# Seven products for the embedding gates too, one bank rule for all panels, and reordered norm ends, experts' loop and third block's start

## The chip, the cores and the metric

The kernel runs on one core of a Trainium2 chip, in fp32. The metric is the device time of one execution, in microseconds. A core has TensorE (PE, matrix products into the 8 banks of PSUM), VectorE (DVE), ScalarE (ACT), GpSimd (POOL), a sync engine (SP) that issues transfers, and 16 DMA engines.

## What is computed

x is 256 tokens by 1024. Three blocks follow each other; cut to what matters here:

```python
# block 1, two layers
for i in range(2):
    mix = ssd_shortconv_layer_mixer(x, ...) if i == 0 else sliding_window_attention(x, ...)
    x = layer_norm(ALPHA * x + mix, ...)
    x = layer_norm(ALPHA * x + (silu(x @ w_gate[i]) * (x @ w_up[i])) @ w_down[i], ...)
    gate = sigmoid(x @ w_ple_gate[i] + b_ple_gate[i])
    x = x + (p[i] @ w_ple[i]) * gate
# block 2: RWKV-7 and stick-breaking attention, then a mixture of 32 experts, 4 for each token
x = x + gate1 * mixed
x = x + gate2 * moe_ffn(rms_norm(x, norm2_g) * (1 + scale2) + shift2, ...)
# block 3: two kinds of attention behind one input projection
h = rms_norm(x, g_pre) * (1 + scale) + shift
proj = h @ w_in
...
```

## The kernel before

x stays in SBUF, transposed: 8 tiles of 128 channels by 256 tokens. The weights are streamed once from HBM. SP brings panels of 1 MB (8 tiles of 128 channels by 256 columns) into a ring of 6 slots, and `linear` (L326) walks over them. A pair of output tiles (256 columns) of a normal panel is 16 products of 128x128 weights by 256 tokens, 8 for each tile, in one bank each; the profile shows a product of fp32 as two records.

**Seven products.** `SevenProducts` (L524 on) computes a panel as a 2x2 block product with seven multiplications in place of eight. Each multiplication is 4 products of 128x128 by 128 tokens (8 records). The order is 1, 5, 7, 6, 2, 3, 4; 1, 6, 5 and 7 go to the four quarters of the panel's first bank, 2, 3 and 4 to the second. GpSimd makes four sums of weights for a panel (`sums`, L585 to L590), VectorE four differences of activations (`turn`, L596 to L601), ScalarE copies the first quarter (L606), and VectorE combines: L612, L613 and L615 from the first bank, L618 from the second, which counts `combined` up. Only then are the two banks free. This form is used for ffn_up (22 pairs, the first one of each layer normal) and ffn_dn (3 panels of input channels for each of 4 pairs), in both layers. `wait_bank` (L374 on) waits, ahead of the first product of a panel, for both of its banks. The banks of a seven-product panel came from a table:

```python
SETS = ((0, 1), (2, 6))
bank = seven.SETS[n % 2][c] if seven is not None and pairs[q][0] in seven.names else (2 * q + c) % banks
```

with banks = 3 in the first block. The embedding gates, ple_g0 and ple_g1 (4 pairs each), use normal products.

**Order around a norm.** `linear` advances other programs between its tiles: what a program yields is the tile behind which it goes on. `LayerNorm` (L1085) follows the tiles of ffn_dn: VectorE adds x0 to x4 (L1168), TensorE sums them over the partitions by a product with ones, VectorE centers by this first mean (L1175, L1178, L1180), ScalarE squares (L1148), and behind the last pair VectorE adds x5 + x6 (L1184) and reduces six squares (L1186), before the last tile's addition (L1114). TensorE sums (L1127 to L1137) and VectorE reads the mean (L1190), then scales by L1204.

**The experts.** `mixture_of_experts` (L2745) works on one expert at a time, 12 panels of 1 MB: 8 that widen (L3071) and 4 that narrow (L3101), as 6 pairs. Pairs lie in 8 slots: the first TWICE = 2 pairs of an expert have a slot for even and one for odd experts, the other four have one. A turn of the TensorE loop is: widen u, scatter u-1, gather u+2, narrow u. Scattered results are added by VectorE to `acc` (L2840, 4 additions of 512 columns). While the routing is computed TensorE ends with idle products of a constant (L2870). Behind the last expert `ClosingNorm` (L2681) adds gate times `acc` to x (L2697) and makes the sum of squares for the third block.

**Third block.** `third_block` (L3606) waits for the finished norm: `NormTail` scales (L268) and shifts (L274) the 8 tiles into h, and `linear` starts behind each.

## Time and profile before

| | before |
|---|---|
| median of 3 runs | 2394.82 us (2394.03 to 2396.35) |
| profiled execution, its own time | 2397.78 us |
| its span, first to last instruction | 2395.9 us |
| granted TensorE clock, mean | 0.987 of full speed |
| TensorE busy | 2261.8 us, 94% |
| HBM read | 616.63 MB, 258 GB/s over the span |

The span is the profiler's; the device time of the same execution is 1.9 us longer, and sums are made against that. The first block lasts until about 920, the second until 2130, of which the experts take 1198 to 2120, and the third to the end. In rows of stretches the number behind each busy time is a count of instructions. In a timeline a gap in brackets is the engine's idle time before the row, with what ended it. Granted clock 1.00 is 2.4 GHz.

### The profile page before, as it was taken

To read this page: it belongs to the slowest core of one execution; us is meant where nothing else is said; L and a number is where in the kernel's file an instruction comes from. 1 tells how busy PE (TensorE), PEld (TensorE's weight loads), DVE (VectorE), ACT (ScalarE), POOL (GpSimd) and SP (SyncE) were. 2 spreads that over 40 slices of the span, in tenths; PEclk is the share of its full clock that TensorE was granted. 3 is DMA by queue.
4 is the path that set the end of the run, shared out by engine and by line. 5 is a ranking of instruction groups with operands and counts; after the bars stand their busy time and mean duration, and the time that the engine had idled before them with its cause. 6 is when DMAs were issued, how large, how long until landed. Compare 5 with 4: busy or idle time off the path is not lost. (4 is left out here: it accounts for less than half of the span.)

```text
span 2395.9 us, 35084 instructions
## 1 busy us (share of the span) xinstructions
PE 2261.8 (94%) x14543; PEld 1537.5 (64%) x14543; DVE 890.1 (37%) x1790; ACT 419.3 (18%) x898; POOL 417.1 (17%) x343
## 2 busy tenths in 40 slices
PE   8999999989899989999999999999999999989998
PEld 7888799977699977877733333333333333358886
DVE  4242565634444653626422222222322222253222
ACT  1210121014211013224111111111111111123331
POOL 0110498700088830011000000000000000000000
PEclk9999899999999989999999999999999999999999
DMA  6334644454854444310699999999999999943322
GB/s 263 132 124 141 213 167 160 163 191 181 317 211 161 160 170 154 124 37 2 283 376 428 428 428 428 428 428 428 428 428 428 428 428 428 428 194 124 143 71 88
DMA packets 61005, 619.28 MB, mean 258 GB/s; under 512 B 6784, under 2 KB 8064, under 8 KB 12288
## 3 DMA queue, kind: packets, MB, share of 16 engines
q1 hardware_dynamic: 59184, 611.08, 63.9%
q10 hardware_dynamic: 1712, 6.63, 0.8%
q8 instruction: 83, 1.36, 0.2%
q14 instruction: 26, 0.21, 0.0%
HBM read 616.63 MB, written 1.05 MB: 258 GB/s over the span
## 5 line engine op out<-in xcount | busy, mean ns | idle before, releaser
L431 PE MATMUL ps<-x_res,ring 128*128 128x256 f32 x1216 | 284.2, 393 | 24.0 <-ACT x_res L1157 15.4
L431 PEld LDWEIGHTS ps<-x_res,ring 128*128 128x128 f32 x1216 | 236.3, 197 | 64.8 <-issue 16.8
L3071 PE MATMUL ps<-expert_ring,moe_xg 128*64 128x512 f32 x1024 | 229.0, 594 | 25.7 <-DMA expert_ring<-we_dram 25.7
L3071 PE MATMUL ps<-ring,moe_xg 128*64 128x512 f32 x1024 | 227.9, 594 | 5.1 <-DMA ring<-we_dram 5.1
L3101 PE MATMUL ps<-expert_ring,mix_y 128*64 128x512 f32 x1024 | 226.8, 596 | 0.0
L3133 DVE TENSOR_SCALAR mix_y<-ps 128x512 f32<-128x512 f32 x32 | 22.1, 691 | 454.5 <-PE ps L3071 454.5
L3389 POOL COPY third_mla_kv<-third_lat 32x256 f32<-32x256 f32 x8 | 3.5, 457 | 1055.4 <-ACT third_mla_kv L658 1055.3
L3071 PEld LDWEIGHTS ps<-expert_ring,moe_xg 128*64 128x64 f32 x1024 | 71.5, 137 | 172.2 <-issue 124.6
L431 PE MATMUL ps<-third_h,ring 128*128 128x256 f32 x768 | 176.6, 387 | 5.2 <-ACT third_h L274 4.3
L3071 PEld LDWEIGHTS ps<-ring,moe_xg 128*64 128x64 f32 x1024 | 72.0, 137 | 150.9 <-issue 125.1
L431 PEld LDWEIGHTS ps<-third_h,ring 128*128 128x128 f32 x768 | 148.0, 194 | 28.1 <-issue 6.6
L3101 PEld LDWEIGHTS ps<-expert_ring,mix_y 128*64 128x64 f32 x1024 | 70.5, 137 | 133.4 <-issue 133.4
L3114 ACT ACTIVATE mix_y<-mix_y 128x512 f32<-128x512 f32 x32 | 20.2, 630 | 695.6 <-DVE mix_y L3133 695.6
L431 PE MATMUL ps<-mix_arena,ring 128*128 128x256 f32 x416 | 96.2, 389 | 4.3 <-ACT mix_arena L274 4.3
L586 POOL TENSOR_TENSOR ring<-ring 128x512 f32<-128x512 f32 (+1 forms) x66 | 99.9, 1514 | 0.0
L585 POOL TENSOR_TENSOR seven_weights<-ring 128x512 f32<-128x512 f32 (+1 forms) x66 | 86.0, 1304 | 71.8 <-PE ps L414 64.3
L431 PEld LDWEIGHTS ps<-mix_arena,ring 128*128 128x128 f32 x416 | 79.7, 194 | 17.3 <-issue 6.1
L588 POOL TENSOR_TENSOR seven_weights<-seven_weights,ring 128x512 f32<-128x512 f32 (+1 forms) x66 | 90.2, 1366 | 0.0
L414 PE MATMUL ps<-x_res,ring 128*128 128x128 f32 x672 | 89.0, 276 | 0.0
L414 PE MATMUL ps<-seven_x_turned,ring 128*128 128x128 f32 x672 | 88.8, 275 | 0.0
L414 PE MATMUL ps<-seven_x_turned,seven_weights 128*128 128x128 f32 x672 | 88.8, 275 | 0.0
L3148 DVE COPY moe_ytok<-ps 128x512 f32<-128x512 f32 x32 | 22.1, 692 | 176.1 <-PE ps L3101 176.1
(592 smaller groups left out, 3319.8 us busy)
## 6 DMA issues: line engine op xcount, KB each, us to landing
expert_ring<-we_dram SPq DMA_DIRECT2D x128, 2048.0 KB, 22.0
ring<-we_dram SPq DMA_DIRECT2D x64, 2048.0 KB, 24.5
ring<-w_in_dram SPq DMA_DIRECT2D x55, 1024.0 KB, 4.9
ring<-ffn_up_dram SPq DMA_DIRECT2D x44, 1024.0 KB, 4.9
ring<-ada_dram SPq DMA_DIRECT2D x36, 1024.0 KB, 4.9
ring<-w_out_dram SPq DMA_DIRECT2D x16, 1024.0 KB, 4.9
ring<-ffn_dn_dram SPq DMA_DIRECT2D x16, 1024.0 KB, 4.9
ring<-ple_g_dram SPq DMA_DIRECT2D x8, 1024.0 KB, 5.6
```

The costliest lines, as they stand in the source:

```text
L414: mm = pe.matmul(core.ps[:, bank, at:at + P], seven.weight(w, f, half, product, p), seven.moving(panel, sources[panel], k0, half, product, ...
L431: mm = pe.matmul(core.ps[:, bank_of[n, c], 0:TOK], w[:, k * PANEL + c * P:k * PANEL + c * P + P], sources[panel](k0 + k), start=(k0 + k == ...
L585: pool.tensor_tensor(s1, a21, a22, ALU.add).then_inc(summed.sem, 1)
L586: pool.tensor_tensor(a21, a11, a21, ALU.subtract).then_inc(summed.sem, 1)
L588: pool.tensor_tensor(s2, s1, a11, ALU.subtract).then_inc(summed.sem, 1)
L3071: mm = pe.matmul(ps[out, bank, :], xg[:, j % 4, j // 4, :], w[:, bank * D + at:bank * D + at + 512], start=False, stop=(j == 7))
L3101: mm = pe.matmul(ps[out, 2, :], hidt[:, at_k:at_k + S], w[:, i * D + at:i * D + at + 512], start=False, stop=(k == DT - 1))
L3114: act.activation(sg[:, :], glu[:, :], ACT.Sigmoid, scale=SWIGLU_ALPHA).then_inc(sig_ready.sem, 1)
L3133: dve.tensor_scalar(glu[:, :], ps[:, 0, :], SWIGLU_LIMIT, None, ALU.min).then_inc(glu_ready.sem, 1)
L3148: dve.tensor_copy(ytok[:, :], ps[:, 2, :]).then_inc(copied.sem, 1)
L3389: pool.tensor_copy(kv[64:96, t, :], lat[64:96, 3, :]).then_inc(*inc("keyed"))
```

## The change

- `SETS` is gone. The banks of unit n (a panel by seven products, or a normal pair) are (2n) mod 3 and (2n + 1) mod 3, also in the names with seven products. Where two such panels follow each other, the second bank of the later is the first bank of the earlier.
- Pairs 1 to 3 of ple_g0 and ple_g1 go by seven products, 6 panels, with turned activations of their own.
- GpSimd starts the weight sums of the first fast panel of ffn_up0, ffn_up1, ple_g0 and ple_g1 only when VectorE's four differences are there.
- In the norms of ffn_dn (`split`) the first mean is that of x0 to x3, the reduction of six squares stands behind the centering and no longer behind the last pair, x4 to x7 are summed by TensorE directly, and the five filling products stand together behind them.
- Experts: nine slots of pairs (TWICE = 3) in place of eight (the memory of `acc` goes to it); the results are added straight into x with their gate, in 8 instructions of 256 columns; expert 0 is widened in the routing's block, with the loads for its slots' successors; the loop's turn is narrow u, widen u+1. `widen` and `narrow` have the instructions of the old loop body. `ClosingNorm` is gone.
- Third block: `UnscaledStart`. The first four tiles are computed from x times gain, unscaled (with one more column, the shift, so 257), and multiplied by the root's inverse afterwards by VectorE, then shifted by ScalarE. The sum of squares is four ones products in the middle of the second tile. h for the later tiles is made meanwhile.

```diff
-            bank = seven.SETS[n % 2][c] if seven is not None and pairs[q][0] in seven.names else (2 * q + c) % banks
+            bank = raw.BANKS[2 * q + c] if raw is not None and 2 * q + c < raw.COUNT else (2 * n + c) % banks
...
-                    for k in range(kn):
+                    if raw is not None and t < raw.COUNT:
+                        for m, k in enumerate(raw.ORDER):
+                            raw.before(pe, t, m)
+                            mm = pe.matmul(core.ps[:, bank_of[n, c], 0:raw.WIDTH], w[:, k * PANEL + c * P:k * PANEL + c * P + P], raw.moving(k),
+                                           start=(m == 0), stop=(m == DT - 1))
+                    for k in range(kn if raw is None or t >= raw.COUNT else 0):
+                        if raw is not None and t == raw.COUNT:
+                            raw.wait(pe, k)
...
-    SETS = ((0, 1), (2, 6))
...
+        name, j = core.stream[i][0:2]
+        if j == self.first_pair[name] > 0:
+
+            pool.wait_ge(self.turned.sem, self.turned.at(4 * self.groups[name, 0] + 4))
...
+        if self.split:
+            self.wait(pe, "centered", 2)
+            for t in range(4, 8):
+                if t == 6:
+                    self.wait(pe, "squares_added_up", 1)
+                    pe.matmul(ps[:, 5, 0:TOK], ones, self.run.shift[:, :], start=True, stop=False)
+                if t >= 6:
+                    core.wait_tile(pe, self.first + t)
+                mm = pe.matmul(ps[:, 4, TOK:], ones, x[:, t, :], start=(t == 4), stop=(t == 7))
+            mm.then_inc(*self.inc("mean"))
+            for t in (6, 7):
+                self.wait(pe, "squared", t - 3)
+                mm = pe.matmul(ps[:, 5, 0:TOK], ones, sq[:, t, :], start=False, stop=(t == 7))
+            mm.then_inc(*self.inc("power"))
+            self.fill(pe, 5)
+            return
...
+        summed = 4 if self.split else 5
+        for t in range(1, summed):
+            yield self.first + t
+            core.wait_tile(dve, self.first + t)
+            add = dve.tensor_tensor(run.offset[:, :], x[:, 0, :] if t == 1 else run.offset[:, :], x[:, t, :], ALU.add)
+            if t < summed - 1:
...
+        if self.split:
+            self.wait(dve, "squared", 2)
+            dve.tensor_reduce(run.shift[:, :], run.sq[:, 0:6, :].rearrange("p t n -> p n t"), AX,
+                              ALU.add).then_inc(*self.inc("squares_added_up"))
+        yield self.first + 6
+        if not self.split:
+            self.add_last(dve)
...
+        turn_order = [("ffn_up0", 0), *(("ffn_dn0", k0) for k0 in range(0, FF_T, KG)), ("ple_g0", 0),
+                      ("ffn_up1", 0), *(("ffn_dn1", k0) for k0 in range(0, FF_T, KG)), ("ple_g1", 0)]
+
+        def groups(name):
+            return {k0: n for n, (of, k0) in enumerate(turn_order) if of == name}
+        parts_fast = {name: (1, turned_x, None, groups(name)) for name in ("ffn_up0", "ple_g0", "ffn_up1", "ple_g1")}
...
+class UnscaledStart:
+
+
+    ORDER, BANKS, COUNT, WIDTH = (0, 1, 4, 5, 2, 3, 6, 7), (0, 1, 2, 6), 4, TOK + 1
+    SUM_BANK = 7
...
+    def before(self, pe, t, n):
+        if t == 0:
+            if n == 0:
+                self.at(pe, "columns", 1)
+            self.at(pe, "gained", n + 1)
+        if (t, n) == (1, 4):
+            self.at(pe, "halved", 1)
+            for i in range(4):
+                mm = pe.matmul(self.core.ps[:, self.SUM_BANK, 0:TOK], self.core.m("ones"), self.sq[:, i, :], start=(i == 0), stop=(i == 3))
+            mm.then_inc(*self.inc("summed"))
...
+        for k in self.ORDER:
+            part = core.ps[:, 2 + k // 2, k % 2 * TOK:k % 2 * TOK + TOK]
+            dve.scalar_tensor_tensor(out=x[:, k, :], in0=part, scalar=gate[:, k:k + 1], in1=x[:, k, :], op0=ALU.mult,
+                                     op1=ALU.add).then_inc(*self.inc("kept"))
+        self.at(dve, "kept", DT)
+        dve.tensor_tensor(sq[:, 0:4, :], x[:, 0:4, :], x[:, 0:4, :], ALU.mult).then_inc(*self.inc("squared"))
+        self.at(dve, "squared", 2)
+        dve.tensor_tensor(sq[:, 0:4, :], sq[:, 0:4, :], sq[:, 4:8, :], ALU.add).then_inc(*self.inc("halved"))
+        self.at(dve, "summed", 1)
+        dve.tensor_scalar(rstd[:, :], core.ps[:, self.SUM_BANK, 0:TOK], 1.0 / D, RMS_EPS, ALU.mult, ALU.add).then_inc(*self.inc("var"))
+        self.at(dve, "rooted", 1)
+        dve.reciprocal(rstd[:, :], rstd[:, :]).then_inc(*self.inc("inverse"))
+        self.at(dve, "inverse", 1)
+        for t in range(self.COUNT):
+            if t == 2:
+                for half in range(2):
+                    part = slice(4 * half, 4 * half + 4)
+                    dve.tensor_tensor(self.out[:, part, :], self.xg[:, part, 0:TOK], bcast(rstd[:, :].unsqueeze(1), [P, 4, TOK]),
+                                      ALU.mult).then_inc(*self.inc("h_scaled"))
+            core.wait_product(dve, t)
+            bank = core.bank_of_tile(t)
+            dve.tensor_copy(self.added[:, t:t + 1], core.ps[:, bank, TOK:TOK + 1])
+            dve.tensor_tensor(self.first_tiles[t], core.ps[:, bank, 0:TOK], rstd[:, :], ALU.mult).then_inc(*self.inc("scaled"))
...
+        for n, k in enumerate(self.ORDER):
+            self.at(act, "kept", n + 1)
+            act.activation(self.xg[:, k, 0:TOK], x[:, k, :], ACT.Copy, scale=core.gain[:, k:k + 1]).then_inc(*self.inc("gained"))
+        act.activation(self.sq[:, 4:8, :], x[:, 4:8, :], ACT.Square).then_inc(*self.inc("squared"))
+        self.at(act, "var", 1)
+        act.activation(core.rstd[:, :], core.rstd[:, :], ACT.Sqrt).then_inc(*self.inc("rooted"))
...
-                part = acc[:, 4 * i + 2 * q:4 * i + 2 * q + 2, :]
                 dve.wait_ge(scattered.sem, scattered.at(u * 4 + (n + 1)))
-                dve.tensor_tensor(part, part, ps[:, 2 + 2 * i + q, :].rearrange("p (k n) -> p k n", n=TOK),
-                                  ALU.add).then_inc(added.sem, 1)
+                for t in range(2):
+                    k = 4 * i + 2 * q + t
+                    ins = dve.scalar_tensor_tensor(out=x[:, k, :], in0=ps[:, 2 + 2 * i + q, t * TOK:t * TOK + TOK], scalar=gate[:, k:k + 1],
+                                                   in1=x[:, k, :], op0=ALU.mult, op1=ALU.add)
+                ins.then_inc(added.sem, 1)
...
-                    keep_busy(12)
+                    widen(pe, 0, 0, 0)
...
+                    load(sp, 0, twice, 0, 2)
+                    load(sp, 0, opened, 1, 1)
...
+                load(sp, 0, range(4, PAIRS), 1, 1)
+                load(sp, 1, twice, 1, 3)
+                load(sp, 1, once, 0, 2)
+                with sp.Fori(2, AHEAD) as v:
+                    load(sp, v * 2 - 2, twice, 0, v * 2)
+                    load(sp, v * 2 - 2, once, 1, v * 2 - 1)
+                    load(sp, v * 2 - 1, twice, 1, v * 2 + 1)
+                    load(sp, v * 2 - 1, once, 0, v * 2)
...
+                last = last_pair(pe)
+                with pe.Fori(0, last) as v:
+                    narrow(pe, v * 2, v, 0)
+                    widen(pe, v * 2 + 1, v, 1)
+                    narrow(pe, v * 2 + 1, v, 1)
+                    widen(pe, v * 2 + 2, v + 1, 0)
+                narrow(pe, last * 2, last, 0)
+                widen(pe, last * 2 + 1, last, 1)
+                narrow(pe, last * 2 + 1, last, 1)
+                scatter(pe, last * 2 + 2)
...
-PANELS, PAIRS, TWICE, AHEAD = 12, 6, 2, 9
...
+PANELS, PAIRS, TWICE, AHEAD = 12, 6, 3, 9
...
-        norm = NormTail(core, h, x, lambda k: core.gain[:, k:k + 1], lambda k: shift[:, k:k + 1])
+        start = UnscaledStart(core, s, h, [lat[:, m, :] for m in range(4)])
```

Three places show the new order. The first is TensorE at ple_g0, in the second of its pairs (`x_res` is x, `seven_x_turned` the differences, `seven_weights` the sums, `ring` the panel). The columns are line, operation, output<-inputs, shape, what it waits for, and how often it comes. Before:

```order
L431 MATMUL ps<-x_res,ring 128x256 [waits seven_combined,panel_loaded3]
L431 MATMUL ps<-x_res,ring 128x256 x7
L431 MATMUL ps<-x_res,ring 128x256 [waits act_evac]
L431 MATMUL ps<-x_res,ring 128x256 x7
```

With the change:

```order
L424 MATMUL ps<-x_res,ring 128x128 [waits seven_combined,act_evac,panel_loaded4]
L424 MATMUL ps<-x_res,ring 128x128 x3
L424 MATMUL ps<-seven_x_turned,seven_weights 128x128 [waits seven_summed]
L424 MATMUL ps<-seven_x_turned,seven_weights 128x128 x3
L424 MATMUL ps<-seven_x_turned,ring 128x128 [waits seven_summed]
L424 MATMUL ps<-seven_x_turned,ring 128x128 x3
L424 MATMUL ps<-seven_x_turned,seven_weights 128x128 [waits seven_summed]
L424 MATMUL ps<-seven_x_turned,seven_weights 128x128 x3
L424 MATMUL ps<-x_res,ring 128x128 x4
```

Sixteen products of 256 tokens have become seven groups of four; the wait for the combination stands at the first product, while the second bank is first written by the fifth group (`x_res` with `ring`, x4 in one row). Inside ffn_up and ffn_dn the rows read the same before and after, only the count that `seven_combined` must have reached is that of the panel before, no longer of the one before that.

The second is VectorE at the end of ffn_dn0, from the last combination that the first mean comes before to the reading of the mean. Before:

```order
L1175 TENSOR_SCALAR ln_shift<-ps 128x256 [waits layer_signal28,dve_evac]
L1178 TENSOR_TENSOR x_res<-x_res,ln_shift 128x768 [waits dve_chain]
L1178 TENSOR_TENSOR x_res<-x_res,ln_shift 128x768
L1180 SCALAR_TENSOR_TENSOR x_res<-x_res,ln_shift 128x512
L612 TENSOR_TENSOR seven_second<-seven_part,ps 128x128 [waits seven_copied,dve_chain]
L613 TENSOR_TENSOR seven_part<-seven_second,ps 128x256 [waits dve_chain]
...
L1114 TENSOR_TENSOR x_res<-x_res,seven_stage 128x256 [waits seven_combined]
L1184 TENSOR_TENSOR ln_offset<-x_res 128x256 [waits layer_signal29,dve_evac]
L1186 TENSOR_REDUCE ln_shift<-ln_sq 128x256 [waits layer_signal30]
L1114 TENSOR_TENSOR x_res<-x_res,seven_stage 128x256 [waits seven_combined]
L1190 TENSOR_SCALAR ln_offset<-ps 128x256 [waits layer_signal31]
```

With the change:

```order
L1225 TENSOR_SCALAR ln_shift<-ps 128x256 [waits layer_signal28,dve_evac]
L1228 TENSOR_TENSOR x_res<-x_res,ln_shift 128x768 [waits dve_chain]
L1228 TENSOR_TENSOR x_res<-x_res,ln_shift 128x768
L1230 SCALAR_TENSOR_TENSOR x_res<-x_res,ln_shift 128x512
L1233 TENSOR_REDUCE ln_shift<-ln_sq 128x256 [waits layer_signal30,dve_chain]
L633 TENSOR_TENSOR seven_second<-seven_part,ps 128x128 [waits seven_copied]
L634 TENSOR_TENSOR seven_part<-seven_second,ps 128x256 [waits dve_chain]
...
L1137 TENSOR_TENSOR x_res<-x_res,seven_stage 128x256 [waits seven_combined] x2
L1240 TENSOR_SCALAR ln_offset<-ps 128x256 [waits layer_signal31]
```

The reduction (L1186, now L1233) has moved ahead of the combination of the first panel of the last pair, and the addition of x5 and x6 (L1184) is gone.

The third is TensorE from the end of the routing to the experts' loop. Before:

```order
L2909 MATMUL ps<-route_onehot,mat 1x17
L2870 MATMUL ps<-mat 128x128 [waits layer_signal26]
L2870 MATMUL ps<-mat 128x128 x11
L2858 UNCONDITIONAL_BRANCH
L3050 UNCONDITIONAL_BRANCH [waits barrier_Pool_Activation_PE_DVE_SP_release]
L2776 TENSOR_LOAD moe_unit_int
L2776 ISA x2
...
L3066 MATMUL ps<-bias_parts,moe_pick 64x512 [waits expert_xg_ready,expert_expert_picked]
L3066 MATMUL ps<-bias_parts,moe_pick 64x512 x3
```

With the change:

```order
L3076 MATMUL ps<-route_onehot,mat 1x17
L2951 MATMUL ps<-bias_parts,moe_pick 64x512 [waits layer_signal26,expert_xg_ready,expert_expert_picked]
L2951 MATMUL ps<-bias_parts,moe_pick 64x512 x3
L2956 MATMUL ps<-ring,moe_xg 64x512 [waits expert_pair0]
L2956 MATMUL ps<-ring,moe_xg 64x512 x7
...
L2956 MATMUL ps<-expert_ring,moe_xg 64x512 [waits expert_pair3]
L2956 MATMUL ps<-expert_ring,moe_xg 64x512 x7
L3022 UNCONDITIONAL_BRANCH
L3209 UNCONDITIONAL_BRANCH [waits barrier_Pool_Activation_PE_DVE_SP_release]
L2876 TENSOR_LOAD moe_unit_int
...
L2931 MATMUL ps<-moe_selt,moe_ytok 128x256 [waits expert_added]
```

The idle products (L2870) have become the widening of expert 0 (4 pairs, 8 products each), and the loop begins with a scatter (L2931).

## Rows read from the trace of the kernel before

**Rows 1.** The page, busy time of each engine.

```profile
PE 2261.8 (94%) x14543; PEld 1537.5 (64%) x14543; DVE 890.1 (37%) x1790; ACT 419.3 (18%) x898; POOL 417.1 (17%) x343
```

**Rows 2.** Windows: stretch, length, busy of each engine, PEclk, DMA share, GB/s.

```profile
275.00:406.00 131.00, 131.00 (x1175) 130.97 (x1174) 67.11 (x114) 24.89 (x45) 112.55 (x80) 1.00 0.49 168
1300.00:1400.00 100.00, 97.36 (x489) 35.91 (x489) 26.49 (x63) 11.03 (x16) 0.00 (x0) 1.00 1.01 428
458.00:461.00 3.00, 0.29 (x3) 0.14 (x2) 2.75 (x4) 0.00 (x0) 3.00 (x3) 1.00 0.55 161
461.00:465.00 4.00, 4.00 (x20) 3.95 (x21) 3.93 (x4) 0.81 (x1) 3.92 (x3) 0.57 0.34 141
1190.00:1210.00 20.00, 17.07 (x104) 9.60 (x106) 4.73 (x23) 2.11 (x3) 0.00 (x0) 1.00 0.46 177
2120.00:2126.40 6.40, 4.51 (x16) 2.53 (x16) 5.07 (x11) 3.25 (x8) 0.00 (x0) 1.00 0.34 140
```

**Rows 3.** The chain that ended last: start us, us, engine, line, count.

```profile
2151.15 13.81 PE ps L431 x64
```

**Rows 4.** Timeline, ffn_up0: start us, us, engine, line, op, names, shapes, count.

```profile
400.14 1.06 PE L414 MATMUL ps<-x_res,ring 128*128 128x128 f32 x8
400.34 0.56 DVE L618 TENSOR_TENSOR seven_stage<-seven_part,ps 128x384 f32<-128x384 f32 x1 [1.24 <-PE ps L414]
406.39 1.06 PE L414 MATMUL ps<-first_arena,ring 128*128 128x128 f32 x8
```

**Rows 5.** Timeline, norm at the end of ffn_dn0.

```profile
481.01 0.42 DVE L1114 TENSOR_TENSOR x_res<-x_res,seven_stage 128x256 f32<-128x256 f32 x1
481.81 2.74 DVE L1186 TENSOR_REDUCE ln_shift<-ln_sq 128x256 f32<-128x1536 f32 x1
484.60 0.70 PE L1132 MATMUL ps<-ln_shift,mat 128*128 128x256 f32 x2 [1.96 <-DVE ln_shift L1186]
488.96 0.42 DVE L1190 TENSOR_SCALAR ln_offset<-ps 128x256 f32<-128x256 f32 x1 [4.08 <-PE ps L1137]
```

**Rows 6.** Timeline, end of the routing and first product of expert 0.

```profile
1193.79 2.95 PE L2870 MATMUL ps<-mat 128*128 128x128 f32 x24
1198.37 0.62 PE L3066 MATMUL ps<-bias_parts,moe_pick 96*64 96x512 bf16 x4 [1.64 <-issue]
```

**Rows 7.** Timeline, middle of ffn_up0 and its step to ffn_dn0.

```profile
368.87 1.06 PE L414 MATMUL ps<-x_res,ring 128*128 128x128 f32 x8
378.35 0.55 DVE L618 TENSOR_TENSOR seven_stage<-seven_part,ps 128x384 f32<-128x384 f32 x1
414.38 0.55 DVE L618 TENSOR_TENSOR seven_stage<-seven_part,ps 128x384 f32<-128x384 f32 x1
```

**Rows 8.** Timeline, centering in ffn_dn0.

```profile
462.70 3.41 DVE L1178 TENSOR_TENSOR x_res<-x_res,ln_shift 128x768 f32<-128x768 f32 x2
```

**Rows 9.** Timeline, scaling ahead of ffn_up0, of ple_g0 and of ffn_up1.

```profile
257.25 10.61 DVE L1204 SCALAR_TENSOR_TENSOR x_res<-x_res,vec,norm_rstd 128x256 f32<-128x256 f32 x8
275.08 1.05 PE L414 MATMUL ps<-x_res,ring 128*128 128x128 f32 x8
494.99 3.25 DVE L1204 SCALAR_TENSOR_TENSOR x_res<-x_res,vec,norm_rstd 128x256 f32<-128x256 f32 x8
504.79 0.47 ACT L659 ACTIVATE first_arena<-ps,vec 128x256 f32<-128x256 f32 x1 [2.98 <-PE ps L431]
653.47 4.27 DVE L1204 SCALAR_TENSOR_TENSOR x_res<-x_res,vec,norm_rstd 128x256 f32<-128x256 f32 x8
```

**Rows 10.** Timeline, end of the experts and start of the third block.

```profile
2117.87 2.00 PE L2831 MATMUL ps<-moe_selt,moe_ytok 64*128 64x256 f32 x16 [0.87 <-DVE moe_ytok L3148]
2119.76 0.88 DVE L2697 SCALAR_TENSOR_TENSOR x_res<-moe_acc,modulations,x_res 128x256 f32<-128x256 f32 x2
2127.36 1.75 DVE L2721 RECIPROCAL norm_rstd<-norm_rstd 128x256 f32<-128x256 f32 x1 [0.48 <-ACT norm_rstd L2707]
2146.44 0.38 ACT L658 ACTIVATE third_lat<-ps 128x256 f32<-128x256 f32 x1 [3.07 <-PE ps L431]
```

323 lines of the change are left out of this document (152 added, 171 removed).

## The prediction, before the change ran

> **What bounds the kernel now.** I read the busy times first: TensorE works 94% of the span, VectorE 37%, GpSimd 17% [rows 1]. So nearly every microsecond that TensorE gains or loses is one of the program, unless TensorE waits for weights. The table of stretches shows the two regimes [rows 2]. In the first block (275 to 406) TensorE is busy 131.00 of 131.00 at clock 1.00 and the DMA share is 0.49: TensorE is the bound, and any wait between two panels is paid in full. In the experts (1300 to 1400) the DMA share is 1.01 at 428 GB/s: the weights are the bound, and work of 2 or 3 us that is moved there costs nothing. The third block (the chain's one run of 64 products, 13.81 us [rows 3]) is TensorE's again. The sum is made against the profiled execution, 2397.78 us; the median of the runs shown, 2394.82, is 2.96 lower. About 0.2%, 4.8 us, is what a measurement can tell from no change.
>
> **A, the banks.** A panel by seven products fills two banks. Before, two neighbours had four different banks, so TensorE waited for the combination of the panel before last. Now the second bank of a panel is the first of the panel before it, and both waits stand ahead of the first product. The next panel starts at 400.14, but VectorE's last combination of the panel before starts only at 400.34 and takes 0.56 [rows 4]. So each boundary gets 0.20 + 0.56 = 0.76, plus the way of the signal from VectorE to TensorE, 0.05 (a reduction of 2.74 from 481.81 ends at 484.55, the product that waits for it starts at 484.60 [rows 5]), plus a first weight load that nothing hides: two products alone take 0.70 there, where in a run of 24 each takes 2.95 / 24 = 0.12 at 128 columns [rows 5, 6]; I estimate 0.10. That is 0.9 each; bounds 0.75 (signal and load hidden) and 1.05 (both doubled). Boundaries: per layer 20 inside ffn_up, 1 to ffn_dn, 11 inside ffn_dn and 2 between the new gate panels, 34; two layers 68, less one that the modulation work hides in ffn_up1: 67 × 0.90 = **+60.3**.
>
> **B, VectorE late.** In the middle of ffn_up VectorE also turns half of the hidden vector, ahead of the combination. There the combination ends at 378.35 + 0.55 = 378.90, 10.03 after the panel began at 368.87 [rows 7]; with signal and load 10.18. A panel takes 6.25 (400.14 to 406.39 [rows 4]), and the next would now end its own stall at 0.90 + 6.25 = 7.15. TensorE stands still 3.0, of which 0.90 is counted: 2.1, four times, **+8.4**. At the step to ffn_dn the combination ends at 414.93, 8.54 after 406.39 [rows 4, 7]: 8.69 − 7.15 = 1.54, of which 0.64 is new, twice, **+1.3**.
>
> **C, the clock.** Behind the stretch 458 to 461, where TensorE worked 0.29 of 3 us, the next 4 us run at a granted clock of 0.57: 0.43 × 4 = 1.7 lost [rows 2]. I charge this to the four stalls of 3.0: **+6.8**, bounds 0 and 6.8.
>
> **D, the norm at the end of ffn_dn.** VectorE's sums of squares move from the last slot to the one before. Centering starts 1.7 into the panel (462.70 [rows 8], the panel at 461.0 [rows 2]) and takes 3.41; then the two late tiles (a third more, 1.1), what is left of the squares on ScalarE (0.25, estimated), the reduction of 2.74 [rows 5], the combination (1.2 and 0.55) and the signal, 0.15: 11.1, and the panel is over at 6.25. That stall is 4.9 instead of 0.9: 4.0 more, and 1.7 of clock; what goes is the old wait for the fifth tile, 2.7 and its 1.7 of clock [rows 2]. Twice +1.3: **+2.6**. What it buys comes at the very end. The last tile's addition starts at 481.01, the reduction then holds VectorE for 2.74 and TensorE starts behind it at 484.60; the mean is read at 488.96 [rows 5]. Now the last addition ends near 481.9, two ones products remain (0.6) and the mean is read near 482.75: 6.2 earlier, twice, **−12.4**. Adding x4 to x7 on TensorE costs nothing on VectorE, whose sums are hidden by TensorE's tiles; if that cover went it would be 0.35 a product, half of the 0.70 of two [rows 5].
>
> **E, the gates.** Six panel pairs go from 32 products at 13.81 / 64 = 0.216, 6.91 [rows 3], to 6.25 [rows 4]: 0.66 each, **−4.0**. Their turning on VectorE lies under the normal first pair, GpSimd's first sum behind it; both are there before the second product. Were they late, TensorE would wait for them on VectorE's and GpSimd's time, and GpSimd is idle there.
>
> **F, weight sums wait for the activation sums.** At ffn_up0 the scaling starts at 257.25, takes 10.61 beside GpSimd's sums, and the first fast panel starts at 275.08, 17.8 later. At ple_g0, with GpSimd idle, it takes 3.25 from 494.99, and the pair's last product ends just ahead of the evacuation at 504.79, 9.6 later [rows 9]. So **−8.2** there; in ffn_up1 the scaling took 4.27 [rows 9], 0.8 more than it must, **−0.8**. The sums themselves start later, under the normal pair of 6.91, and are needed only one product, 6.25 / 7 = 0.89, into the fast one; that cover is what hides them.
>
> **G, the experts.** From 1190 to 1210 the DMA share is 0.46 [rows 2]: 20 × 0.54 = 10.8 us of a bandwidth-bound phase not used, because the ring was full and freed only once the first expert was widened. A ninth pair of panels (2 MB at 428 GB/s, 4.9) can be loaded in that time, and widening starts where the idle products were, 4.4 to 4.6 earlier (1193.79 against 1198.37 [rows 6]), so slots free 4.4 earlier. Of the hole 1.6 stays; and since loads of expert 1 beyond the fourth pair wait for expert 0's narrowing, behind a barrier, a hole of about 2.7 opens: 10.9 − 4.3 = **−6.6**, bounds −3 and −10.9. Adding eight 256-column parts straight into x instead of four of 512 costs VectorE about 0.9 an expert, hidden by the DMA-bound loop (VectorE works 26.49 of 100 there [rows 2]); without that cover 32 × 0.9 = 29.
>
> **H, third block.** The last scatter (2117.87, 2.00) ends at 2119.87, and the fourth tile's product ends at about 2146.25, just ahead of its evacuation [rows 10]. Now: barrier 0.4, eight residuals of 0.44 (0.88 for two [rows 10]) to 2123.8; the unscaled products follow and tile 0 ends near 2125.8; three tiles of 3.46 (6.91 / 2) and four ones products, 1.73 (4 × 2 × 0.216), to 2138.0; the reciprocal (1.75 [rows 10]) runs beside them. With 1.9 for a slow clock behind the pause (0.43 × 4 as in C, rounded up, since the pauses are several), 2139.9: **−6.3**, bounds −4 and −7.5.
>
> **Sum:** 60.3 + 8.4 + 1.3 + 6.8 + 2.6 = 79.4; −12.4 −4.0 −9.0 −6.6 −6.3 = −38.3; net +41.1. 2397.78 + 41.1 = 2438.9, less 2.96: **2436**.
>
> **Rivals.**
> - *The boundary wait is hidden (faster).* The shared bank is written by the fifth of seven products only, 3.6 us in. If the wait did not hold the first product (the combination frees the bank earlier than the rows say, or products already queued cover it), A, B and C go: −38.3, 2356. It decides at 38.3 / 67 = 0.57 a boundary with B and C gone, or 0.29 with them. Against it: the order of instructions has the wait on the first product; [rows 4] give at least 0.76. Chance 0.04.
> - *The clock falls at every boundary.* An idle of 2.7 cost 1.7 afterwards [rows 2]. If 0.9 did so too, 67 × 1.7 = 114: 2550. Against it: from 2120 to 2126.4 TensorE worked only 4.51 of 6.40, in short pauses between its ones products, and the clock stayed 1.00 [rows 2]. The Trainium skill (TensorE: Matmul & The Clock Gate, A second HAM failure mode: psum-queue depth-cycling) tells of a kernel whose TensorE "micro-idles between MM groups" while it cycles through banks, and whose clock then oscillates; by it this rival would be the forecast. The stretch just quoted does not follow that rule, though it is only 6 us long. Chance 0.08.
> - *The repairs don't do what they are for.* The experts' start is bound by something else than the ring, and the third block's start by its pauses: G and H are 0, 2449. Chance 0.06.
>
> **How the numbers follow.** The forecast has 0.80; 0.02 is left for what I don't see. The low end takes A at 0.75 (−10), C at 0 (−6.8), G and H at their best (−5.5) and F and E exact: about 2412 with 2 for B. The high end takes A at 1.05 (+10), G and H at their worst (+5.9), and the norms' gain 3 less each (+6): 2458, rounded to 2460; the third rival lies inside. Left out are the clock (0.08), the hidden wait (0.04) and the rest. Slower by over 0.2%: 0.80 + 0.08 + 0.06 = 0.94; faster 0.04, same 0.02.
>
> **What the changed profile must show.** At each fast panel in ffn_up a wait of TensorE of about 0.9 on VectorE's last combination, some 67 times, and TensorE's busy share there at 0.87 instead of 1.00; four idles of 3.0 and two of 4.9 with a clock of about 0.6 behind them; the mean of ffn_dn's norm read 6 us sooner after the last product; the first scaling of ffn_up0 in 3.3; a DMA share near 0.8 in the 20 us before the experts' loop; the fourth tile of the third block 20 us behind the last scatter, not 26.4. I am wrong if TensorE runs through the boundaries, or if the clock is below 0.9 all through ffn_up.

## The result, and the profile after

The changed kernel takes **2439.19 us** in the median of 4 runs (2437.22 to 2441.01), the kernel before 2394.43 on the same chip: ratio 1.0187, 95% interval 1.017 to 1.0205, 44.8 us slower. Forecast: 2436, range 2412 to 2460. The profiled execution took 2439.19 (span 2437.4), 41.4 more than the profiled one of before; the sum had said 41.1.

Busy time of the engines on the page of after (span first), against [rows 1]:

```profile
span 2437.4 us, 35516 instructions
## 1 busy us (share of the span) xinstructions
PE 2256.9 (93%) x14663; PEld 1541.6 (63%) x14663; DVE 910.1 (37%) x1946; ACT 420.9 (17%) x905; POOL 437.7 (18%) x367
```

TensorE's busy time fell by 5 us while the span grew by 41.5: what was added is waiting. What TensorE waited for (columns: in total, times, longest):

```profile
engine line waited for: us in total, times, longest us
PE ps L424 <- DVE seven_stage L639: 63.1, 67, 5.1
PE ps L2956 <- DMA expert_ring<-we_dram: 25.0, 19, 1.6
```

The first line does not exist in the kernel before. 67 times is the number that the prediction counted; 52 of the waits are 0.74 long, the others 0.3 to 5.1. One boundary inside ffn_up0, and the one in the middle where VectorE is late (timeline, columns as in [rows 4], some rows between left out):

```profile
372.54 0.29 DVE L636 TENSOR_TENSOR seven_stage<-seven_part,ps 128x128 f32<-128x128 f32 x1
372.97 1.06 PE L424 MATMUL ps<-seven_x_turned,ring 128*128 128x128 f32 x8
374.07 0.55 DVE L639 TENSOR_TENSOR seven_stage<-seven_part,ps 128x384 f32<-128x384 f32 x1 [1.24 <-PE ps L424]
374.77 1.13 PE L424 MATMUL ps<-x_res,ring 128*128 128x128 f32 x8 [0.74 <-DVE seven_stage L639]
375.73 1.06 PE L424 MATMUL ps<-seven_x_turned,seven_weights 128*128 128x128 f32 x8
...
383.07 1.13 PE L424 MATMUL ps<-x_res,ring 128*128 128x128 f32 x8 [1.81 <-DVE seven_stage L639]
...
390.30 1.13 PE L424 MATMUL ps<-x_res,ring 128*128 128x128 f32 x8 [0.74 <-DVE seven_stage L639]
```

Without a wait the next panel would start 0.89 behind the last group, at 373.86. VectorE begins its last combination 0.21 later, needs 0.55, TensorE starts 0.15 behind its end, and the first group then takes 0.07 more (0.96 to the next, not 0.89): 0.98 for a boundary. Panels now come every 7.23 (383.07 to 390.30), not every 6.25 [rows 4]. The late one in the middle has 1.81 in place of 0.74.

The first row shows something more. L636 (L615 before) is the last instruction that reads the panel's first bank, the one that the next panel needs again. It ends at 372.83, a microsecond ahead of 373.86. What TensorE waits for is the counter `combined`, which goes up only behind the combination from the other bank.

That late place came out earlier than forecast. Of VectorE's four differences there, the last one and what GpSimd did beside it, before and after:

```profile
375.44 1.46 POOL L585 TENSOR_TENSOR seven_weights<-ring 128x512 f32<-128x512 f32 x1 [0.21 <-PE ps L414]
375.81 1.65 DVE L601 TENSOR_TENSOR seven_h_turned<-first_arena,seven_h_turned 128x512 f32<-128x512 f32 x1
```

```profile
380.80 0.69 DVE L622 TENSOR_TENSOR seven_h_turned<-first_arena,seven_h_turned 128x512 f32<-128x512 f32 x1
381.40 1.26 POOL L606 TENSOR_TENSOR seven_weights<-ring 128x512 f32<-128x512 f32 x1 [1.19 <-PE ps L424]
```

It takes 1.64 or 1.65 in all four such places of the kernel before, and 0.69 in all four of the changed one. At the place shown GpSimd now stands idle for 1.19, until TensorE has finished a panel whose buffer its sums need.

Stretches of after (columns as in [rows 2]):

```profile
266.00:410.00 144.00, 127.82 (x1107) 124.75 (x1106) 62.18 (x108) 24.40 (x43) 113.71 (x83) 1.00 0.45 151
384.00:390.00 6.00, 5.56 (x50) 5.37 (x49) 1.57 (x5) 0.28 (x1) 2.87 (x3) 1.00 0.24 102
486.80:491.90 5.10, 0.03 (x1) 0.00 (x0) 4.62 (x7) 0.85 (x2) 4.00 (x4) 1.00 0.58 206
491.95:495.95 4.00, 4.00 (x21) 4.00 (x22) 0.58 (x1) 0.00 (x0) 0.00 (x0) 0.57 0.02 4
801.40:805.40 4.00, 4.00 (x25) 4.00 (x26) 0.65 (x1) 0.22 (x1) 3.36 (x3) 0.66 0.48 203
2171.32:2175.32 4.00, 4.00 (x11) 3.21 (x12) 2.46 (x5) 3.60 (x8) 0.00 (x0) 0.57 0.08 30
```

ffn_up0 is busy 127.82 of 144 with the clock at 1.00 throughout, also behind the 1.81 us stall (384 to 390). It falls to 0.57 behind the 5.12 us stall in ffn_dn's last pair, and behind the pause of 2.99 ahead of the third block. It also falls behind one of the four late stalls, the second of ffn_up1, to 0.66:

```profile
801.32 1.13 PE L424 MATMUL ps<-x_res,ring 128*128 128x128 f32 x8 [2.10 <-DVE seven_stage L639]
...
810.17 1.13 PE L424 MATMUL ps<-x_res,ring 128*128 128x128 f32 x8 [0.74 <-DVE seven_stage L639]
```

This panel takes 8.85 instead of 7.23, 1.6 more. The long stall and the norm's end (timeline):

```profile
487.59 2.78 DVE L1233 TENSOR_REDUCE ln_shift<-ln_sq 128x256 f32<-128x1536 f32 x1 [0.38 <-ACT ln_sq L1187]
...
491.25 0.55 DVE L639 TENSOR_TENSOR seven_stage<-seven_part,ps 128x384 f32<-128x384 f32 x1
...
491.95 1.95 PE L424 MATMUL ps<-first_arena,ring 128*128 128x128 f32 x8 [5.12 <-DVE seven_stage L639]
493.68 1.92 PE L424 MATMUL ps<-seven_h_turned,seven_weights 128*128 128x128 f32 x8
...
505.76 0.55 DVE L639 TENSOR_TENSOR seven_stage<-seven_part,ps 128x384 f32<-128x384 f32 x1 [0.57 <-PE ps L424]
...
508.00 0.42 DVE L1240 TENSOR_SCALAR ln_offset<-ps 128x256 f32<-128x256 f32 x1 [0.89 <-PE ps L1160]
```

The mean is read 2.24 behind the start of the last combination; before it was 8.54 (the combination L618 started at 480.42, the mean is in [rows 5]). 6.3 us are won at each of the two ends.

The scaling ahead of ffn_up0 and ffn_up1, and the first fast panels behind them, against [rows 9] (and 663.42 for ffn_up1 before):

```profile
257.19 3.26 DVE L1254 SCALAR_TENSOR_TENSOR x_res<-x_res,vec,norm_rstd 128x256 f32<-128x256 f32 x8
...
265.35 1.05 PE L424 MATMUL ps<-x_res,ring 128*128 128x128 f32 x8
...
672.32 3.25 DVE L1254 SCALAR_TENSOR_TENSOR x_res<-x_res,vec,norm_rstd 128x256 f32<-128x256 f32 x8
...
682.99 1.16 PE L424 MATMUL ps<-x_res,ring 128*128 128x128 f32 x8
```

8.16 from scaling to panel in ffn_up0 (17.83 before), 10.67 in ffn_up1 (9.95 before).

The start of the third block, against [rows 10]:

```profile
2166.34 2.00 PE L2931 MATMUL ps<-moe_selt,moe_ytok 64*128 64x256 f32 x16 [0.87 <-DVE moe_ytok L3261]
...
2171.32 7.13 PE L439 MATMUL ps<-unscaled_x,ring 128*128 128x257 f32 x24 [2.99 <-ACT unscaled_x L2808]
...
2180.02 8.85 PE L439 MATMUL ps<-unscaled_x,ring 128*128 128x257 f32 x40
...
2188.70 3.62 PE L448 MATMUL ps<-third_h,ring 128*128 128x256 f32 x16
```

The fourth tile is done where the first product with h starts, at 2188.70. That is 20.4 behind the end of the last scatter (2166.34 + 2.00), where the forecast was 20.0; before it was 26.4. So 6.0 are won there. From the start of the scatter to the end of the span it is 271.1 us, before 278.0: 7.0 won.

From the first gather of the routing (1187.66 before, 1238.11 after) to the last scatter it is 930.2 before and 928.2 after: the turned loop with its ninth pair has won 2.0. The two kernels stand 50.5 apart at that gather, 48.5 at the scatter and 41.5 at the end.

### The profile page after: what moved, and what is told of

It is laid out like the page before. It is cut to its first block and busy times, and to the rows that moved or that the text cites. A ratio compares the mean times of both kernels' runs of the same rounds, so it can differ in the third digit from the quotient of the medians.

```text
span 2437.4 us, 35516 instructions
## 1 busy us (share of the span) xinstructions
PE 2256.9 (93%) x14663; PEld 1541.6 (63%) x14663; DVE 910.1 (37%) x1946; ACT 420.9 (17%) x905; POOL 437.7 (18%) x367
## 5 line engine op out<-in xcount | busy, mean ns | idle before, releaser
L2956 PE MATMUL ps<-expert_ring,moe_xg 128*64 128x512 f32 x1280 | 283.4, 594 | 25.3 <-DMA expert_ring<-we_dram 25.0
L448 PE MATMUL ps<-x_res,ring 128*128 128x256 f32 x1024 | 235.1, 389 | 18.9 <-ACT x_res L1196 10.3
L448 PEld LDWEIGHTS ps<-x_res,ring 128*128 128x128 f32 x1024 | 198.0, 196 | 49.3 <-issue 14.0
L2956 PEld LDWEIGHTS ps<-expert_ring,moe_xg 128*64 128x64 f32 x1280 | 89.8, 137 | 208.7 <-issue 160.4
L2956 PE MATMUL ps<-ring,moe_xg 128*64 128x512 f32 x768 | 170.1, 598 | 0.2
L448 PE MATMUL ps<-third_h,ring 128*128 128x256 f32 x704 | 160.1, 383 | 1.3 <-DVE third_h L3740 1.0
L448 PEld LDWEIGHTS ps<-third_h,ring 128*128 128x128 f32 x704 | 134.1, 192 | 21.2 <-issue 2.2
L424 PE MATMUL ps<-x_res,ring 128*128 128x128 f32 x768 | 104.8, 280 | 36.0 <-DVE seven_stage L639 36.0
L2956 PEld LDWEIGHTS ps<-ring,moe_xg 128*64 128x64 f32 x768 | 55.3, 138 | 106.3 <-issue 100.3
L424 PEld LDWEIGHTS ps<-x_res,ring 128*128 128x128 f32 x768 | 93.5, 192 | 43.8 <-issue 43.6
L2941 DVE SCALAR_TENSOR_TENSOR x_res<-ps,modulations,x_res 128x256 f32<-128x256 f32 x256 | 102.9, 474 | 0.0
L424 PE MATMUL ps<-first_arena,ring 128*128 128x128 f32 x528 | 74.2, 283 | 27.1 <-DVE seven_stage L639 27.1
```

The costliest lines, as they stand in the source:

```text
L424: mm = pe.matmul(core.ps[:, bank, at:at + P], seven.weight(w, f, half, product, p), seven.moving(panel, sources[panel], k0, half, product, ...
L448: mm = pe.matmul(core.ps[:, bank_of[n, c], 0:TOK], w[:, k * PANEL + c * P:k * PANEL + c * P + P], sources[panel](k0 + k), start=(k0 + k == ...
L2941: ins = dve.scalar_tensor_tensor(out=x[:, k, :], in0=ps[:, 2 + 2 * i + q, t * TOK:t * TOK + TOK], scalar=gate[:, k:k + 1], in1=x[:, k, :], ...
L2956: mm = pe.matmul(ps[out, bank, :], xg[:, j % 4, j // 4, :], w[:, bank * D + at:bank * D + at + 512], start=False, stop=(j == 7))
```

## The experiments

**The wait alone.** TensorE waits for the second bank only where it is first written:

```diff
                     wait_bank(pe, n, 0)
-                    wait_bank(pe, n, 1)
...
                     for product in seven.ORDER:
+                        if product == 2:
+                            wait_bank(pe, n, 1)
```

> The changed kernel, but TensorE waits for a panel's second bank only ahead of the fifth of its seven products, the first that writes it. Theory (the wait at the first product is the cost): the combination ends 0.76 after the panel's start and the fifth product comes 3.6 after it, so the 67 stalls of 0.74, the four late ones of 1.8 to 2.1 and most of the two of 5.1 at ffn_dn's last pair go; the bank rule itself costs nothing. 67 x 0.98 = 65.7, 6 for the late ones and about 7 for the two long ones: 2439 - 79 = 2360, and a panel takes 6.25 again. Rival (the three banks themselves are too few, since VectorE must read a bank while TensorE fills the next one): the stall moves to the fifth product and the time stays above 2400.

Measured: 2361.30 (2359.98 to 2363.79), ratio to before 0.9846 (0.9829 to 0.9862). Three waits are left of the 67:

```profile
PE ps L425 <- DVE seven_stage L640: 5.1, 3, 2.4
```

and the stretch of ffn_up0 is full again:

```profile
266.00:390.00 124.00, 123.93 (x1103) 123.46 (x1102) 63.81 (x106) 23.93 (x42) 113.11 (x82) 1.00 0.53 173
```

So the place of the wait cost 78 us, and with three banks and this wait the changed kernel is faster than the one before. The shared bank still costs something. The two longest of the three waits, 2.35 and 2.37, stand ahead of the fifth product in ffn_dn's last pair, where VectorE's reduction has come in between, and the clock falls behind them (timeline, then the stretch):

```profile
463.13 1.16 PE L425 MATMUL ps<-first_arena,ring 128*128 128x128 f32 x8 [2.35 <-DVE seven_stage L640]
464.13 1.75 PE L425 MATMUL ps<-first_arena,seven_weights 128*128 128x128 f32 x8
```

```profile
463.13:467.13 4.00, 4.00 (x23) 4.00 (x24) 1.67 (x4) 0.28 (x1) 0.00 (x0) 0.65 0.00 0
```

Another remedy was not tested: the wait left where it is, but for a signal of its own behind the last instruction that reads the first bank (372.83 in the rows above), in place of `combined`.

**Four banks.** The table of before in the changed kernel, for all names with seven products:

```diff
-            bank = raw.BANKS[2 * q + c] if raw is not None and 2 * q + c < raw.COUNT else (2 * n + c) % banks
+            bank = (raw.BANKS[2 * q + c] if raw is not None and 2 * q + c < raw.COUNT else
+                    ((0, 1), (2, 6))[n % 2][c] if seven is not None and pairs[q][0] in seven.names else (2 * q + c) % banks)
```

> The changed kernel with the old table of four banks for all names with seven products. Theory: what remains are the other parts, without any boundary: -65.7 for the stalls, -6 for the late ones, and the two long stalls at ffn_dn's last pair go whole (11.1 against 12.5 of two panels), 2 x 6: about 2355, a little under the late wait. Rival (the clock or VectorE's later work bounds these stages anyway): above 2390.

Measured: 2352.72 (2350.04 to 2355.28), ratio 0.9816 (0.9799 to 0.9832). TensorE waits for no combination. That is 8.6 us below the late wait on the same chip. In ffn_dn0's last pair, from its first product to the product with ones behind it, it is 21.44 us with the late wait and 17.22 here: 4.2 for the stall of 2.35 and its clock, in two layers 8.4. The same kernel once more, on the chip of the last group of runs:

> The changed kernel with four banks once more, on the chip of the three others, as their reference: 2353, between 2350 and 2357. If it falls outside of that, the differences to the runs on another chip are read with that error.

Measured: 2354.63 (2353.73 to 2356.98), ratio 0.9822 (0.9806 to 0.9839). No version of the study is measurably faster; it is 43 us below the kernel before (2397.67 on that chip) and 85 below the changed one. It is the base of the experiments that follow, called the base.

**The banks alone.** The kernel before, with one edit:

```diff
-            bank = seven.SETS[n % 2][c] if seven is not None and pairs[q][0] in seven.names else (2 * q + c) % banks
+            bank = (2 * n + c) % banks
```

> The kernel before with nothing changed but the bank rule, (2n + c) mod 3 for all panels. Theory: 63 boundaries (no fast gates) at 0.98, 61.7, and 6 for the late combinations, so 2394 + 68 = 2462, panels of 7.23. Rival (the stalls come from the other edits, the moved reduction and the weight sums that wait): near 2394.

Measured: 2467.34 (2466.41 to 2470.36), before 2397.38, +70.0; ratio 1.0289 (1.0272 to 1.0306).

```profile
PE ps L414 <- DVE seven_stage L618: 51.0, 61, 1.8
```

The stalls need neither the moved reduction nor the late sums. The loss was forecast at 68; 61 waits were found where 63 were expected.

**Weight sums at once.** The base, without GpSimd's new wait:

```diff
-        if j == self.first_pair[name] > 0:
-
-            pool.wait_ge(self.turned.sem, self.turned.at(4 * self.groups[name, 0] + 4))
```

> The changed kernel with four banks, but GpSimd does not wait for the activation sums. Theory: +9.7 at ffn_up0 where the scaling takes 10.6 again beside GpSimd, -0.7 at ffn_up1, and new overlaps of the same kind ahead of the fast gates in both layers, up to 7 each: between 2362 and 2376, 2369 if half of them overlap. Rival (the start of ffn_up0 is bound by ScalarE's shift or the weights and not by VectorE): within 2 us of 2353.

Measured: 2372.27 (2371.88 to 2377.90), 17.6 to 19.6 above the two runs of the base. The group of the scaling, of the changed kernel and of this one (columns: total busy, mean ns, idle before):

```profile
L1254 DVE SCALAR_TENSOR_TENSOR x_res<-x_res,vec,norm_rstd 128x256 f32<-128x256 f32 x32 | 13.0, 479 | 0.1
```

```profile
L1252 DVE SCALAR_TENSOR_TENSOR x_res<-x_res,vec,norm_rstd 128x256 f32<-128x256 f32 x32 | 33.0, 1100 | 0.1
```

One of them takes at least 472, in the median 1483 and at most 1533 ns (minimum, median and maximum):

```profile
L1252 DVE SCALAR_TENSOR_TENSOR x_res<-x_res,vec,norm_rstd x32: 472/1483/1533, 257.4 to 874.6; 128x256 f32<-128x256 f32 x32
```

The Trainium skill (SBUF — State Buffer, SBUF: two separate sides) says that a VectorE instruction with two inputs in SBUF and one of GpSimd that reads SBUF exclude each other for a whole instruction. The trace agrees: 1483 ns is about the length of one of GpSimd's additions, 1.45 us at this place.

In all the 32 instructions make 33.0 instead of 13.0 us of busy time, since with fast gates GpSimd sums beside the scaling at all four norms: the eight instructions take 9.99, 7.32, 7.35 and 8.32 instead of 3.26. At the two norms ahead of the gates that is 9.1 more, and the fast gates win 4 to 7 (below). By this estimate fast gates without the wait would be a loss; normal gates without it were not run.

**Norm ends of before**, in the base (the class `LayerNorm` of the kernel before; no other edit):

> The changed kernel with four banks and the norm ends of the kernel before. Theory: with four banks VectorE's moved work stalls nobody, so the norm ends are worth their whole gain here, twice 6.3 at the end plus 2.4 for the wait on the fifth tile and 1.7 of clock: 2353 + 21 = 2374. Rival (the moved reduction costs elsewhere what it saves): +13 or less, below 2366.

Measured: 2375.80 (2374.04 to 2378.34), 21.2 to 23.1 above the base. The whole gain is there once nobody waits for VectorE's moved work.

**Normal gates**, in the base (ple_g0 and ple_g1 taken out of the names with seven products, with their turns):

> The changed kernel with four banks and normal products for the embedding gates. Theory: six pairs at 6.91 instead of 6.25, +4.0: 2357. Rival (turning and sums around the gates cost what the seventh product saves): no change beyond 1.5 us.

Measured: 2359.77 (2354.64 to 2363.61). 5 to 7 above the base where 4.0 were expected; its runs spread over 9 us, so this confirms the sign, not the size.

**Loads in one order.** The changed kernel, with SP's order of the first loop in all loops:

```diff
                 def in_turn(v, before, even, odd):
-                    load(sp, v * 2 - 2, once, 1, before)
                     load(sp, v * 2 - 2, twice, 0, even)
-                    load(sp, v * 2 - 1, once, 0, even)
+                    load(sp, v * 2 - 2, once, 1, before)
                     load(sp, v * 2 - 1, twice, 1, odd)
+                    load(sp, v * 2 - 1, once, 0, even)
```

> The changed kernel, but SP issues the experts' loads in one order (three pairs with two slots first) through all loops; the changed kernel switches to the other order at expert 18, where the DMA share falls to 0.89 over 20 us at 1730. Theory: that hole is the switch, with three pairs held back behind one that is late; without it -2.5 to -2.9, 2436.5. Rival (an unrelated pause of the DMA engines): no change beyond 1 us, and a hole somewhere.

Measured: 2449.06 (2443.16 to 2454.97): slower by 10, the expectation was wrong. The stretch of the old hole, in the changed kernel and then here, and the end of the loop here:

```profile
1730.00:1750.00 20.00, 20.00 (x96) 6.53 (x92) 2.24 (x9) 0.00 (x0) 0.00 (x0) 1.00 0.89 365
```

```profile
1730.00:1750.00 20.00, 18.48 (x95) 6.61 (x91) 3.86 (x8) 0.63 (x1) 0.00 (x0) 1.00 1.00 426
2140.00:2170.00 30.00, 28.95 (x146) 10.51 (x142) 8.52 (x22) 2.42 (x4) 0.00 (x0) 1.00 0.82 344
```

The hole is indeed the switch, since it is gone (share 1.00). But it buys something: in this order the next expert's first three pairs are loaded ahead of the last three of the present one, TensorE still waits 1.5 for a pair of the last but one expert, and behind it the engines run dry (0.82) while TensorE works alone. From the first gather to the last it is 924.0 us, in the changed kernel 917.1. (This trace had the faster first widening, of which below; beside a trace with the same, the base's first with 914.3, it is 9.7 more.)

**The switch elsewhere.** The base with `AHEAD` = 3 (expert 6) and with `AHEAD` = 14 (expert 28), in place of 9 (expert 18):

> The changed kernel with four banks, and the experts' loads change their order at expert 6 instead of expert 18. Theory (the lead of three pairs has to be given back somewhere; a hole of 2.9 us at the switch is the price of the ninth pair, and it is the same wherever the switch stands once the slots are full): no change beyond 1.5 us, 2353, with the hole near expert 6. Rival (near the start the DMA engines wait for slots anyway, so that the two holes fall together): -2 to -3, 2350.

Measured: 2359.58 (2352.01 to 2363.06), 5 to 7 above the base, its fastest run level with it: neither the theory nor the rival. The trace is that of the fastest run. The hole came later than at the start, and larger than at expert 18 (31% of 20 us, 6.2; by the bytes, 261 instead of 428 GB/s, 7.8):

```profile
1280.00:1300.00 20.00, 19.33 (x102) 7.54 (x100) 8.19 (x21) 2.42 (x4) 0.00 (x0) 1.00 0.69 261
```

> The changed kernel with four banks, and the loads change their order at expert 28. At expert 18 the switch left a hole of 2.9 us, at expert 6 one of 6.2, with no switch at all 7 us were lost at the end. Theory (TensorE needs 27.6 us for an expert and its weights 29.4, so the lead that SP's order has built up shrinks by 1.8 an expert until it is all used, and what is left at the switch is the hole): the hole is 2.9 at most, so 0 to -1.5, 2352. Rival (the lead does not shrink): a hole of 2.9 to 6 late in the loop, 2353 to 2356.

Measured: 2354.30 (2352.19 to 2357.43), the base's 2354.63 within 0.4; a hole of about 2.7 (409 GB/s instead of 428 over 60 us from 1900; the hole at expert 18 is 2.9 when counted so, 365 over 20 us). So the hole is smaller at expert 18 than at 6, and not clearly smaller at 28. The place chosen, expert 18, is as good as any of the three. Why the hole stays near 2.8 us was not followed up.

**What each half is worth.** The base with experts and third block's start of the kernel before; and the kernel before with the changed experts and start alone:

> The changed kernel with four banks, but the experts and the third block's start are those of the kernel before: what the first block's repairs are worth alone, and by difference to the kernel with four banks what experts and start are worth. Theory from the traces: experts 4.9 (914.3 against 919.2 us from the first gather to the last), start 7.0, so 2353 + 12 = 2365. Rival (the two only shift waits to where the next stage pays them): within 4 us of 2353.

Measured: 2363.11 (2361.25 to 2366.15), 34.6 below the kernel before on that chip.

> The kernel before with the changed experts and third block's start alone. Theory: the parts add, so 2 to 5 for the experts and 7.0 for the start: between 2383 and 2386. Rival (the gains of the two halves depend on each other): outside 2380 to 2390.

Measured: 2387.62 (2386.48 to 2388.74), 10.1 below it; ratio 0.9962 (0.9948 to 0.9976). 34.6 + 10.1 = 44.7, and the base is 43.0 below: the halves add. The start is worth 7 to 8.5 of the 8.5 to 10.1 by the traces (last gather to the end: 289.0 before, 282.2 in the changed kernel, 280.5 in the base), which leaves the experts 0 to 3. From the first gather to the last scatter it is 930.2 us before, 928.2 in the changed kernel, 925.5 and 931.5 in the two traces of the base, and 931.2 in the kernel before with the changed experts. So the experts' edit wins at most 4.7, and in two of these four traces it loses 1.

Why so little: the 52 us behind the first gather, in the kernel before, in the changed one, and in the base on two chips:

```profile
1187.70:1239.70 52.00, 48.28 (x258) 21.08 (x258) 14.06 (x49) 4.90 (x7) 0.00 (x0) 1.00 0.79 324
```

```profile
1238.10:1290.10 52.00, 47.53 (x228) 18.66 (x230) 14.58 (x52) 4.90 (x7) 0.00 (x0) 0.93 0.88 359
1244.10:1250.10 6.00, 6.00 (x23) 2.57 (x24) 1.65 (x10) 0.00 (x0) 0.00 (x0) 0.52 0.58 240
```

```profile
1153.40:1205.40 52.00, 47.54 (x250) 18.94 (x250) 16.12 (x55) 5.53 (x8) 0.00 (x0) 1.00 0.93 383
1159.40:1165.40 6.00, 6.00 (x33) 2.16 (x34) 1.66 (x10) 0.00 (x0) 0.00 (x0) 1.00 0.80 281
```

```profile
1154.30:1206.30 52.00, 47.85 (x216) 18.93 (x218) 14.57 (x52) 4.90 (x7) 0.00 (x0) 0.87 0.82 335
1160.30:1166.30 6.00, 5.89 (x22) 2.96 (x24) 1.82 (x11) 0.00 (x0) 0.00 (x0) 0.54 0.59 246
```

Idle time of the DMA engines is 52 × (1 − share): 10.9 before, 6.2 after, 3.6 in the first trace of the base and 9.4 in the second. The base's two traces differ by the granted clock of the first widening, 1.00 against 0.54: the slots that it frees come later, and the ninth slot's gain is mostly gone. All eleven traces with this start agree: the three with a clock of 1.00 there moved 383 to 385 GB/s over these 52 us, the seven with 0.50 to 0.55 moved 334 to 359, and the one with 0.72 moved 361. From the first gather to the last it is 914.3 in the one and 920.4 in the other (before 919.2).

## Why the prediction was right, step by step

All sizes are against the profiled execution of before.

| step | forecast | measured |
|---|---|---|
| A, 67 boundaries | +60.3 (0.90 each) | +65.7 (0.98 each) |
| B, VectorE late | +9.7 | +6.1 |
| C, clock behind the four stalls | +6.8 | +1.6 |
| D, norm: stall and clock | +2.6 | +1.9 |
| D, norm: end | −12.4 | −12.6 |
| E, gates | −4.0 | −4.0 |
| F, weight sums | −9.0 | −9.0 (−9.7, +0.7) |
| G, experts | −6.6 | −2.0 |
| H, third block | −6.3 | −7.0 |
| sum | +41.1 | +40.7, of 41.4 |

About 0.7 us of the 41.4 I did not place. The sum met the measurement by luck too: A came out 5.4 higher, B and C 8.8 lower, and G 4.6 short of its gain.

- **A** held in mechanism and count, which the late wait (−78 us) and the banks alone (+70) show from both sides. Two of its terms were mis-sized: the signal from VectorE to TensorE took 0.15, not the 0.05 read off the reduction in [rows 5], and the load was 0.07, not 0.10.
- **B** failed in a duration. I took VectorE's work in the late places from the trace of before: 10.03 us from where the panel would start without a stall to the end of the combination. There the last of its four differences takes 1.65 beside a sum of GpSimd. In the changed kernel it takes 0.69, since the longer panels leave GpSimd idle at that point, and the combination ends 9.07 behind 373.86 (at 382.93). Measured: 1.8 of idle time in three of four places and 2.10 in the fourth, not 3.0.
- **C** shrank with it. Behind the three stalls of 1.8 the granted clock stayed 1.00; only behind the one of 2.10 did it fall, and that cost 1.6, near the 1.7 that each was priced at. The rival of a falling clock is refuted: with pauses of 0.74 every 7.23 us the clock stayed 1.00 over 144 us in ffn_up0, and over 74 us in ffn_dn0 behind it (412 to 486). The Trainium skill (TensorE: Matmul & The Clock Gate, A second HAM failure mode: psum-queue depth-cycling) tells of a kernel in which such idles between groups make the clock oscillate. This kernel's idles of 0.74 do not; its pauses of 2.10, 2.99 and 5.12 us were followed by 0.66, 0.57 and 0.57.
- **D** was right on both sides: a stall of 5.12 (4.9) with the clock behind it, and 6.3 (6.2) at the end. The 1.9 is read from the panels: from the end of the group ahead of the first-mean product to the end of the last group it is 22.24 before and 26.13 after, less three boundaries of 0.98, twice. What it didn't say is that the stall is a child of A: with four banks it vanishes and the edit is worth 21 to 23 us.
- **E** can be seen only where no boundary is paid: the three fast panels of a layer take 20.7 us, as three normal pairs did (20.7), since two boundaries of 0.98 eat the 3 × 0.66. In the books that is −4.0 in E and 4 × 0.98 in A.
- **F** came out at the sum by two errors that cancel: 9.7 at ffn_up0 instead of 8.2 (the estimate was borrowed from ple_g0, whose first pair runs partly at a lower clock), and a loss of 0.7 in ffn_up1 instead of a gain of 0.8, where the pair now takes 8.6 us in place of 7.8. Both are the clock's doing. The first normal pair of ffn_up0 took 7.14 here, at 1.00; in the traces of the late wait and of the base's second run it took 8.83, at 0.65 and 0.66 over its first 4 us, behind the same pause of 3.2. In ffn_up1 the clock over 4 us near the pair's start was 0.75, before it was 1.00.
- **G** is the step that failed most. The hole of the start was put at 4.3 and is 6.2, with a clock of 0.52 at the first widening; at clock 1.00 it is 3.6 (first trace of the base), near the forecast. And the hole of 2.9 where SP changes its order was not seen at all: the DMA share of the kernel before shows none. That kernel lets two pairs lead instead of three, which would explain it; that is not shown, since a loop with nine slots and no lead was not tried.
- **H** was right: the fourth tile came 20.4 behind the end of the scatter, forecast 20.0, with the slow clock behind the pause that the forecast had in it (0.57 over 4 us). That is 6.0; the other 1.0 came some 100 us later, where both kernels pause for 3.17 us and the clock of the 4 us behind it was 0.50 before and 0.64 now. The edit does nothing there.

The rival of the hidden wait had its price right: with the wait out of the way the kernel takes 2361 and 2353, where it said 2356. It was wrong as a forecast since the code puts both waits ahead of the first product. The third rival (G and H at zero) is refuted as a whole by the kernel before with these two alone, −10.1, but its half on the experts came close: in that run's trace they took 931.2 us, 1.0 more than before.

## What to carry to other kernels

When the number of buffers shrinks, ask not whether the next work has to wait but at which of its instructions: here the shared bank is written in the fifth of seven groups, and moving one wait there turned 45 us of loss into 36 of gain. Ask also whether the signal that it waits for is the one of its own bank. Price a stall that repeats by adding the consumer's start, its length, the signal and the restart, then multiply by a count taken from the order of instructions; for work that comes late, look at what ran beside it when its duration was taken, since a new stall changes that company too. And edits are to be timed on a base without the fault: by the table the norm end was worth some 11 of its 21 us in the changed kernel, and the fast gates nothing.

## What the runs showed of the hardware that was not expected

- The granted clock stayed at 1.00 (2.4 GHz) through 144 us in which TensorE paused 0.74 every 7.23 us, and behind pauses of 1.8. Behind one of 2.10 it was 0.66 over 4 us, behind one of 5.12 0.57, with groups 1.73 apart instead of 0.89, the lower level of 1.2 GHz.
- The length of the pause alone does not settle it. Ahead of ffn_up0 TensorE pauses for 3.2 us: in the changed kernel's trace the clock of the next 4 us was 1.00, in those of the late wait and of the base's second run 0.65 and 0.66, and the same 32 products took 7.14 and 8.83 us.
- At the end of the routing, where the same products run in every version, the clock of the next 6 us was 1.00 in one trace of the base and 0.54 in the other. With it the experts' part went from 914.3 to 920.4 us, through the DMA engines, which wait for slots that TensorE frees.
- VectorE's scaling instruction of 256 columns took 479 ns on average with GpSimd idle and 1100 ns on average when GpSimd summed weights beside most of them, with no semaphore between the two. VectorE's difference of 512 columns took 1.65 us beside GpSimd's sum and 0.69 without.
